# A PEER encoder on one Trainium2 core: the picks' source moved, all side dots in the projection, fewer whole blocks in the second expert product

## The reference, cut to what matters

```
s  = einsum('thpd,pnd->thpn', (x @ w_q), sub_keys)     # 8 heads x 2 sides x 128 keys
sv, si = top_k(s, 16)                                  # and 16 of the 16 x 16 sums of both sides
experts, gates = ...                                   # 8 x 16 = 128 experts of 16384 per token
a = gelu(einsum('td,tkd->tk', x, take(u, experts))) * gates
y = einsum('tk,tkd->td', a, take(v, experts))
x = layer_norm(ALPHA * x + y)
```

## Time and profile before

| | |
|---|---|
| median of 3 runs | 1611.62 us (1608.67 to 1612.37) |
| the profiled execution's own time | 1610.4 us |
| its span | 1608.6 us |
| PE busy | 1585.3 us, 99% |
| DVE busy | 1344.9 us, 84% |
| ACT busy | 653.0 us, 41% |
| POOL busy | 594.5 us, 37% |
| DMA | 477.16 MB, mean 297 GB/s |

### The profile page before, as it was taken

How to read it: one execution, slowest core, us unless ns; L and a number is a source line. 1 busy time by engine, 2 the same in 40 slices (tenths; PEclk the granted TensorE clock), 3 DMA queues, 4 the chain that set the end, 5 groups by cost and what they waited for, 6 DMA issues and landing times. The chain is left out here.

```text
span 1608.6 us, 28100 instructions
## 1 busy us (share of the span) xinstructions
PE 1585.3 (99%) x10798; PEld 1529.2 (95%) x10798; DVE 1344.9 (84%) x2545; ACT 653.0 (41%) x1183; POOL 594.5 (37%) x438
## 2 busy tenths in 40 slices
PE   8999999999999999999999999999999999999998
PEld 8988999999999999999888899999999999999996
DVE  6986696899998999898856749969999978888885
ACT  5564221333334444544535341123333344444452
POOL 5651006444433455554003200073443335555510
PEclk9999999999999999999999999999999999999999
DMA  7644468999999999999733237799999999999980
GB/s 249 223 144 148 169 211 270 365 359 353 347 356 352 385 383 399 387 400 372 295 121 118 79 118 247 215 324 375 356 354 348 360 366 379 393 397 394 387 339 26
DMA packets 133381, 477.16 MB, mean 297 GB/s; under 512 B 16576, under 2 KB 17088, under 8 KB 132992
## 3 DMA queue, kind: packets, MB, share of 16 engines
q1 hardware_dynamic: 85248, 307.42, 53.2%
q0 software_dynamic: 43968, 153.27, 25.0%
q10 hardware_dynamic: 4032, 14.68, 2.6%
HBM read 472.01 MB, written 1.05 MB: 294 GB/s over the span
## 5 line engine op out<-in xcount | busy, mean ns | idle before, releaser
L676 POOL DMA_INDIRECT big<-v,picks x144 | 248.9, 1729 | 224.5 <-DVE big L1908 191.9
L676 POOL DMA_INDIRECT big<-u_rows,picks x144 | 201.8, 1402 | 295.6 <-DVE big L1826 271.6
L710 PE MATMUL work<-columns,raw 128*128 128x184 f32 x1824 | 296.1, 320 | 0.1
L710 PEld LDWEIGHTS work<-columns,raw 128*128 128x128 f32 x1824 | 284.8, 190 | 0.3 <-issue 0.3
L608 DVE TENSOR_TENSOR low<-raw,high 128x1024 fp32r<-128x1024 f32 x192 | 239.9, 1253 | 38.1 <-ACT high L1231 36.2
L1231 ACT ACTIVATE high<-raw 128x1024 fp32r<-128x1024 f32 x208 | 217.4, 1048 | 43.8 <-DMA raw<-v 12.5
L1908 DVE SCALAR_TENSOR_TENSOR big<-big,side_hid 128x1024 f32<-128x1024 f32 x140 | 179.0, 1278 | 1.5
L1826 DVE SCALAR_TENSOR_TENSOR big<-big 128x1024 f32<-128x1024 f32 x144 | 172.0, 1218 | 0.5 <-DMA big<-u_rows,picks 0.5
L1492 ACT ACTIVATE xT<-big 128x184 fp32r<-128x184 f32 x210 | 72.8, 354 | 235.3 <-PE work L855 186.0
L710 PE MATMUL work<-columns,extra_raw 128*128 128x184 f32 x864 | 141.6, 319 | 0.3 <-DMA extra_raw<-u 0.3
L730 PE MATMUL work<-xT,high 128*128 128x368 f32 x704 | 137.5, 337 | 0.8 <-DVE big L1804 0.6
(11 more groups left out here) (258 smaller groups left out, 2869.8 us busy)
## 6 DMA issues: line engine op xcount, KB each, us to landing
raw<-u SPq DMA_DIRECT2D x172, 512.0 KB
raw<-v SPq DMA_DIRECT2D x172, 512.0 KB
extra_raw<-u SPq DMA_DIRECT2D x84, 512.0 KB
extra_raw<-v SPq DMA_DIRECT2D x84, 512.0 KB
raw<-wq SPq DMA_DIRECT2D x32, 512.0 KB
raw<-conv_in SPq DMA_DIRECT2D x14, 512.0 KB
aux<-ln_par ACTq DMA_DIRECT2D x9, 512.0 KB, 9.2
raw<-conv_out SPq DMA_DIRECT2D x8, 512.0 KB
```

The costliest lines, as they stand in the source:

```text
L676: nc.gpsimd.indirect_dma_start(out=side_rows[n % SIDE_BUFS], out_offset=None, in_=rows, in_offset=bass.IndirectOffsetOnAxis(ap=pick_ids[:, ...
L710: mm = nc.tensor.matmul(out_, raw_at(c)[:, k * P:(k + 1) * P], x_full[:, k, :], start=(k == 0), stop=(k == KD - 1))
```

## The change

It does seven things. `own_picks` moves out of the ring into the side columns of `xT` (`beside_xT`), as two halves of 64 picks for ids and for gates. The rooms of the ring and of the side tokens trade places, and `SIDE_BUFS` becomes a formula, whose value is (120 - 92) // 4 - 2 = 5, as before; `gate_scaled` gets another room. The 32 small transfers of the second set are issued one by one behind gathers 8 to 39; behind gather 40 POOL waits for the picks and clears the side columns. All 72 dots of a layer are in the projection: two in each of pairs 1 to 6, the other 60 over pairs 7 to 44. ScalarE's side GELU is at column 2 and the sums run from column 4 to 113. `FULL_V` is every seventh block, 17 a layer. VectorE waits for the query projection's end before it writes `own_picks`.

```diff
@@ -73,18 +73,20 @@
 SET_AT = [P - sum(_n for _n, _ in SETS[:_i + 1]) for _i in range(len(SETS))]
 SIDE_GROUPS = sum(_groups for _, _groups in SETS)
 SIDE_ROWS = sum(SET_ROWS)
-SIDE_BUFS = 5
+SIDE_BUFS = (120 - SIDE_ROOM) // 4 - len(SETS)
 MINE = 0 if SET_AT[-1] < 64 else 64 if SET_AT[-1] < 96 else 96
 BATCHES = DT // BATCH
 PAIR_OF = [_b * (PAIRS - 3) // (BATCHES - 1) for _b in range(BATCHES)]
 BATCH_OF = {_pair: _b for _b, _pair in enumerate(PAIR_OF)}
 FULL_PAIRS = {2, *PAIR_OF}
 MERGED = PAIRS - len(FULL_PAIRS)
+FIRST_DOTS = 12
 DOT_PAIRS = {}
-for _d in range(SET_ROWS[0]):
-    DOT_PAIRS.setdefault(2 + _d * (PAIRS - 4) // SET_ROWS[0], []).append(_d)
-SIDE_DOTS_AT = {2 + _d: SET_ENDS[0] + _d for _d in range(SET_ROWS[1])}
-SIDE_GELU_AT = max(SIDE_DOTS_AT) + 3
+for _d in range(SIDE_ROWS):
+    _at = 1 + _d // 2 if _d < FIRST_DOTS else 7 + (_d - FIRST_DOTS) * (PAIRS - 8) // (SIDE_ROWS - FIRST_DOTS)
+    DOT_PAIRS.setdefault(_at, []).append(_d)
+SECOND_FROM = 8
+SIDE_GELU_AT = 2
 SIDE_STEP = (115 - SIDE_GELU_AT - 2) / SIDE_ROWS
 SIDE_SUMS_AT = {SIDE_GELU_AT + 2 + int(_d * SIDE_STEP): _d for _d in range(SIDE_ROWS)}
 GATE_SCALE = 2.0 ** 15
@@ -123,7 +125,7 @@
     return n < EARLY or n == NKEYS - 1 or late // 2 in FULL_PAIRS
 
 
-FULL_V = [_n for _n in range(FIRST_COLUMNS, COLUMNS - LAST_COLUMNS) if _n % 5 == 3]
+FULL_V = [_n for _n in range(FIRST_COLUMNS, COLUMNS - LAST_COLUMNS) if _n % 7 == 3]
 FULL = {FIRST[f"u{_layer}"] + _n for _layer in range(DEPTH) for _n in range(NKEYS) if whole(_layer, _n)}
 FULL |= {FIRST[f"v{_layer}"] + _n for _layer in range(DEPTH) for _n in FULL_V}
 A_RANK = [sum(_m not in FULL_V for _m in range(_n + 1)) for _n in range(NKEYS)]
@@ -292,7 +294,9 @@
         raw = sb("raw", [P, RAW, D])
         high = sb("high", [P, RING, D], F32R)
         low = sb("low", [P, RING, D], F32R)
+        xT_at = -(-nc.sbuf_base // 32) * 32
         xT = sb("xT", [P, KD, 2, T], F32R)
+        beside_xT = nc.alloc_sbuf_tensor_at("beside_xT", [P, KD, 2, T], F32, offset=xT_at)
         xT_high, xT_low = xT[:, :, 0, :], xT[:, :, 1, :]
         cross = sb("cross", [P, 2, T])
         x = sb("x", [P, HALVES, D])
@@ -320,10 +324,10 @@
 
 
         hid = room(0, NKEYS * DT).rearrange("p (b t) -> p b t", t=DT)
-        side_x = [room(SIDE_ROOM + 4 * n, D) for n in range(len(SETS))]
+        side_x = [room(120 - 4 * (len(SETS) - n), D) for n in range(len(SETS))]
         side_sum = side_x
-        side_rows = [room(SIDE_ROOM + 4 * (len(SETS) + n), D) for n in range(SIDE_BUFS)]
-        own_picks = room(SIDE_ROOM + 4 * (len(SETS) + SIDE_BUFS) - 1, 2 * P).rearrange("p (s k) -> p s k", s=2)
+        side_rows = [room(SIDE_ROOM + 4 * n, D) for n in range(SIDE_BUFS)]
+        own_picks = beside_xT[:, 0:4, 0, DT:DT + P // 2].rearrange("p (s h) k -> p s h k", s=2)
         pick_ids = picks[:, 0, :].bitcast(I32)
         selector = [cross[:, 0, n * P:(n + 1) * P] for n in range(len(SETS))]
 
@@ -353,7 +357,7 @@
         rest = [room(92, NKEYS), room(95, NKEYS)]
         gate_sum = room(94, HALVES * PH)
         gate_inv = room(94, T)[:, P:P + HALVES * PH]
-        gate_scaled = room(90, T)
+        gate_scaled = room(80, T)
 
         cands = room(112, HALVES * PH * CANDS).rearrange("p (j c) -> p j c", c=CANDS)
         rank2 = room(42, 2 * T, F16).rearrange("p (s k d) -> p s k d", s=2, d=2)
@@ -648,25 +652,23 @@
                 pool.wait_ge(xT_lo_ok, split)
                 nc.gpsimd.tensor_tensor(x_full[:], xT_high[:, :, 0:DT].bitcast(F32), xT_low[:, :, 0:DT].bitcast(F32),
                                         ALU.add).then_inc(x_full_ok, 1)
-                pool.wait_ge(block_used, end_of[f"wq{layer}"])
-                nc.gpsimd.memset(xT[:, :, :, DT:T].bitcast(F32), 0.0).then_inc(side_zero, 1)
                 pool.wait_ge(own_picked, layer + 1)
 
-                def fetch_picks(i):
-                    n, groups = SETS[i]
-                    mine, rows, end_row = slice(SET_AT[i], SET_AT[i] + n), SET_ROWS[i], SET_ENDS[i]
-                    for g in range(groups):
-                        at = slice(n * g, n * (g + 1))
-                        nc.gpsimd.dma_start(picks[at, :, end_row - rows:end_row],
-                                            own_picks[mine, :, rows * g:rows * (g + 1)]).then_inc(picks_in[i], 16)
-                fetch_picks(0)
-
-                def fetch_tokens(i):
-                    n, groups = SETS[i]
-                    for g in range(groups):
-                        at = slice(n * g, n * (g + 1))
-                        nc.gpsimd.dma_start(side_x[i][at], x[SET_AT[i]:SET_AT[i] + n, 1, :]).then_inc(side_x_in[i], 16)
-                fetch_tokens(0)
+                def fetch_picks(i, g):
+                    n, rows, end_row = SETS[i][0], SET_ROWS[i], SET_ENDS[i]
+                    half, at = divmod(rows * g, P // 2)
+                    nc.gpsimd.dma_start(
+                        picks[n * g:n * (g + 1), :, end_row - rows:end_row],
+                        own_picks[SET_AT[i]:SET_AT[i] + n, :, half, at:at + rows]).then_inc(picks_in[i], 16)
+
+                def fetch_tokens(i, g):
+                    n = SETS[i][0]
+                    nc.gpsimd.dma_start(side_x[i][n * g:n * (g + 1)],
+                                        x[SET_AT[i]:SET_AT[i] + n, 1, :]).then_inc(side_x_in[i], 16)
+                for g in range(SETS[0][1]):
+                    fetch_picks(0, g)
+                for g in range(SETS[0][1]):
+                    fetch_tokens(0, g)
                 pool.wait_ge(picks_in[0], 16 * SETS[0][1] * (layer + 1))
 
                 def gather(n):
@@ -680,10 +682,14 @@
                     ).then_inc(side_in[n % SIDE_BUFS], 16)
                 for n in range(2 * SIDE_ROWS):
                     gather(n)
-                    if n == SIDE_BUFS - 2:
-                        fetch_picks(1)
-                        fetch_tokens(1)
-                        pool.wait_ge(picks_in[1], 16 * SETS[1][1] * (layer + 1))
+                    i, groups = n - SECOND_FROM, SETS[1][1]
+                    if 0 <= i < groups:
+                        fetch_picks(1, i)
+                    elif groups <= i < 2 * groups:
+                        fetch_tokens(1, i - groups)
+                    elif i == 2 * groups:
+                        pool.wait_ge(picks_in[1], 16 * groups * (layer + 1))
+                        nc.gpsimd.memset(xT[:, :, :, DT:T].bitcast(F32), 0.0).then_inc(side_zero, 1)
                 if layer == 0:
                     pool.wait_ge(block_used, end_of["mla_in"])
                     nc.gpsimd.memset(mask, 0.0).then_inc(pool_fill, 1)
@@ -1831,9 +1837,11 @@
                 u0 = FIRST[f"u{layer}"]
                 dve.wait_ge(chosen_ok, layer + 1)
                 mine = slice(MINE, P)
-                V.scalar_tensor_tensor(own_picks[mine, 0, :].bitcast(I32), chosen[mine, 0, P:T], float(NKEYS),
-                                       chosen[mine, 1, P:T], ALU.mult, ALU.add)
-                V.tensor_copy(own_picks[mine, 1, :], chosen[mine, 2, P:T]).then_inc(own_picked, 1)
+                dve.wait_ge(block_used, end_of[f"wq{layer}"])
+                halves = lambda ap: ap.rearrange("p (h k) -> p h k", h=2)
+                V.scalar_tensor_tensor(own_picks[mine, 0].bitcast(I32), halves(chosen[mine, 0, P:T]), float(NKEYS),
+                                       halves(chosen[mine, 1, P:T]), ALU.mult, ALU.add)
+                V.tensor_copy(own_picks[mine, 1], halves(chosen[mine, 2, P:T])).then_inc(own_picked, 1)
                 low_stage(u0 + EARLY, u0 + EARLY + 2)
                 dve.wait_ge(chosen_mm, layer + 1)
                 twice = [P, BATCHES, BATCH, 2]
@@ -1908,8 +1916,6 @@
                         V.scalar_tensor_tensor(total, rows, weight, total, ALU.mult,
                                                ALU.add).then_inc(side_used, 1)
                 for c in range(v0, end - TAIL):
-                    if c - v0 in SIDE_DOTS_AT:
-                        side_dot(layer, SIDE_DOTS_AT[c - v0])
                     if c - v0 in SIDE_SUMS_AT:
                         side_weighted(SIDE_SUMS_AT[c - v0])
                     if layer == 0 and c - v0 + RING in ANGLES_AT:
```

## The result

The changed kernel takes 1616.24 us (1614.03 to 1619.49, 7 runs) where the kernel before took 1610.77 (1606.96 to 1612.37, 7 runs) on the same chip. The ratio is 1.0041, interval 1.0032 to 1.0051: slower, by more than the 0.2% that a measurement can tell. The forecast was 1610.9, no change.

The account below looks back on a forecast made before the run. TensorE's instruction stream, busy 99%, was taken as the bound, with VectorE close in the late projection. Terms -3.0 + 2.9 + 0.4 - 1.0 = -0.7 gave 1609.7 us profiled, 1610.9 median; range 1607.0 to 1617.5.

Parts of the forecast that it names:

- late gathers: Rival, projection: at 12.0 us a gather, early dots wait for DMA, 7.4 us in all, 1617.9; chance 0.18.
- Whole v blocks: Columns: six fewer whole blocks a layer at 0.25 us each, all on TensorE's path, -3.0 us.
- Waits in the columns: Columns: fewer gathers in the queues shorten TensorE's waits, between 0 and -2.3 us, taken as -1.0.
- Two of the 1.7 us are the last three columns' and stay: Late columns: two waits of 1.7 us were held not to shrink, leaving 2.3 us of waits.
- Dots in the projection: Projection: more neighbouring pairs with two dots make TensorE wait for VectorE, +1.45 us a layer, +2.9 in all.
- later odd pairs 0.05: Projection: the part of the dots' cost given to odd pairs after 38/39, 0.05 us a layer.
- Gathers up front: Projection, pairs 1 to 8: two dots a pair empty the ring faster, +0.4 us for dots waiting on gathers.
- the 10.1 that were worked out: Early projection: the time in us that a second dot's gather has before the dot needs it.
- The 9.9 of the earlier trace: Trace before: one gather's us from issue to data where a dot waited; another there took 12.0.
- What six more low halves cost VectorE in the columns, nothing: Columns: added low halves and slices, 8.7 to 10.5 us a layer, offset by eight dots leaving, 9.2.
- The rivals: Three alternatives: early gathers late, 1617.9 (0.18); TensorE keeps its gain, 1607.5 (0.17); VectorE saturates, 1616.8 (0.05).
- a VectorE that saturates: Rival: +4.1 us a layer in the projection, no relief in the columns, +5.2 in all, 1616.8; chance 0.05.

Follow-up runs that it names:

- e12: e6 with every fifth v block whole up to block 93, the three late whole ones kept, 22 rather than 17 a layer; 1602.93 us, ratio 0.9956.
- e4: The changed kernel with block 115 still whole and ScalarE and VectorE asked for block 121 one column later; 1605.07 us, ratio 0.9965.
- e1: The changed kernel with the old spacing of whole v blocks, every fifth instead of every seventh; 1611.81 us, ratio 1.0016.
- e8: The changed kernel with the second set's 32 small transfers back in one row behind gather 4; 1630.59 us in one run.
- e6: e5 with later requests for the blocks six behind whole blocks 101, 108 and 115; 1599.67 us, ratio 0.9934.
- e7: The changed kernel with a ring of three rooms in place of five; 1706.94 us in one run.
- e5: The changed kernel with its 72 dots spread evenly: one in each even pair from 12 to 40, two in odd ones, pair 43 one; 1612.04 us, ratio 1.0012.

## Why the prediction was wrong

The forecast of 1610.9 us and "within 0.2%" failed. The range held the time, but by luck: its upper end was put there for late gathers, which didn't come. Two terms of the sum failed, both on the columns: whole blocks taken off "all on the path" with no wait reckoned for where the last one stands, and waits that were to shrink by 1.0 us and grew by 4.2.

- **Whole v blocks, -3.0 us "all on the path".** The unit price was right: a whole block comes every 15.93 us (starts 1322.03 and 1337.96 in layer 1), as forecast, and e12 agrees with the price. The step failed in what it left out: it counted the blocks and not where they stand. Moving the last from 113 to 115 put the request for block 121 behind a room that TensorE itself had to free.
- **Waits in the columns, -1.0 us.** This is the step that failed in sign. I read ScalarE's 3.01 us for a block as queues at their limit, from the 389 GB/s of another window. The queues were busy at that wait as well (0.90 at 288 GB/s from 746.80 to 749.80), but its block, 109, takes the room of whole block 103, and SyncE asked for it only at 744.24, just behind column 103. The mechanism was thus already in the kernel before, and the forecast didn't see it. At the wait that decided, in the changed kernel, the share was 0.00 for the four us ahead: the request was late, not the transfer. "Two of the 1.7 us are the last three columns' and stay" was wrong too, since e4 brings them to 0.92. For the columns the two terms gave -4.0 us and the two traces show +4.1. By the starts of the columns the waits grew by 2.3 and 1.9 us where 1.0 less was forecast; the clock added 2.4 and 0.5, of which the sum had nothing; less the 3.0 of the blocks this is the +4.1. Yet the reason given for the term, eight dots fewer, acts: in e1 the waits are 1.7 us shorter, inside the range of 0 to -2.3.
- **Dots in the projection, +2.9 us.** The mechanism was right, with its places: TensorE is late at pairs 22, 34 and 42, by 0.42, 0.65 and 0.21 where 0.4, 0.7 and 0.15 stood. Pairs 6 to 10 cost 0.28 rather than 0.65. The term that was mis-sized is "later odd pairs 0.05": at pair 45 it was 1.09 us, 0.8 more than before. Pair 43 has two dots, and with pair 45 merged with its neighbour VectorE has one low half more to make ahead of it. VectorE's timeline of the changed kernel, behind pair 43, shows the five in a row:

```profile
495.22 1.23 DVE L612 TENSOR_TENSOR low<-extra_raw,high 128x1024 fp32r<-128x1024 f32 x1 [0.79 <-ACT high L1237]
496.36 1.16 DVE L1796 SCALAR_TENSOR_TENSOR big<-y,big 128x968 f32<-128x968 f32 x1
497.44 1.22 DVE L1832 SCALAR_TENSOR_TENSOR big<-big 128x1024 f32<-128x1024 f32 x1
498.58 1.22 DVE L1832 SCALAR_TENSOR_TENSOR big<-big 128x1024 f32<-128x1024 f32 x1
499.72 0.54 DVE L1810 TENSOR_TENSOR big<-work,big 128x368 f32<-128x368 f32 x1
```

  With it the measured sum is 1.57 and 1.96 a layer for the 1.45 forecast.
- **Gathers up front, +0.4 us.** No dot waits for DMA: 0. Without the burst of small transfers the gathers seen take up to 9.6 us, inside the 10.1 that were worked out. The 9.9 of the earlier trace rows is hardly longer; why the other took 12.0 stays open, since it stood behind two more gathers as well as behind the burst. The rival of late gathers did not come; e8 shows it where the burst is left in.
- **What six more low halves cost VectorE in the columns, nothing.** Right but for a little: the waits for a low half grew from 0.5 to 0.9 us, and e6, with the same low halves, waits for slices 2.4 us in five places where the kernel before waited 5.8 in seven.
- **The rivals.** None had this mechanism. That slower had a chance of 0.23 came from late gathers, which did not come, and from a VectorE that saturates, with +4.1 us a layer in the projection; that came out at the 1.6 and 2.0 near the forecast's own 1.45.

## What to carry to other kernels

Where a buffer is freed by its last consumer for some blocks and by their preparation for others, ask for each irregular one which later request takes its room, and in what order the preparing engine stands for that: here one request, moved by one column, was worth 0.8% (0.9965 against 1.0041). Judge a load on an engine by what stands in two neighbouring steps and not by its mean: 72 dots spread evenly cost TensorE no more than 64 did, the same 72 by a rounding formula 1.6 to 2.0 us a layer more. And before a wait for DMA is called bandwidth, look when the load was asked for, and read the DMA share of that very stretch and of the one ahead of it: a mean over both had 0.51 where the parts had 0.00 and 0.75.

## What the runs showed of the hardware

- A wait of TensorE can cost about as much again in its clock: behind 4.18 us of idle time the granted clock was 0.71 over 9.2 us, and 48 matmuls took 2.4 us longer. Behind 1.74 us it was 1.00 in layer 0 and 0.80 in layer 1 of the kernel before, so the wait's length alone doesn't say it; behind 0.92 us in e4 it was 1.00. Over the traces but e7's, the three last columns took 6.76 or 6.77 us behind every wait of 0.92 to 1.64 us, and 8.26 to 9.66 behind every wait of 3.33 to 4.43; behind the same wait of 4.2 us they lost 1.6 us in one layer of e5 and 2.9 in the other.
- An indirect gather of 512 KB took 7.4 to 9.6 us from issue to use in e7 where a dot waited for it, beside SyncE's loads. The changed kernel's list of DMA issues has 8.7 us for its u gathers as a median and 7.1 for a v block of 512 KB: a gather is slower than a plain load, but not by far.
- Small transfers cost the engine that issues them: 32 in a row took POOL 17 us in e8, and the gather behind them went out that much later.
